# Hybrid decoder layer on one core: other places in the engine queues for evacuations, copies, bias splits and gates, and a weight remainder in four instructions

## The reference, cut to what matters

```python
h = rms_norm(x, g_mix[l])
proj = h @ w_in[l] + b_in[l]          # q, k, v, r, g_lr | sq, sk, sv | gate_a, gate_b
log_g = log_sigmoid(g_lr @ w_gla_gate[l] + b_gla_gate[l]) / GLA_TAU
o_a = gla_chunked(gq, gk, gv, log_g)
o_a = o_a * rsqrt(mean(o_a * o_a) + NORM_EPS) * g_gla_head[l]
y_a = (o_a * silu(gr)) @ w_gla_out[l]
y_b = swa_with_sinks(rope(sq), rope(sk), sv, sinks[l]) @ w_swa_out[l]
mixed = sigmoid(gate_a) * y_a + sigmoid(gate_b) * y_b
x = x + mixed @ w_out[l]
x = x + moe_ffn(rms_norm(x, g_ffn[l]), w_router[l], b_router[l], w_e1[l], b_e1[l], w_e2[l], b_e2[l])
return rms_norm(x, g_final)
```

## Time and profile before

| what | us |
|---|---|
| median of 3 runs | 1237.48 |
| lowest, highest | 1231.65, 1239.58 |
| profiled execution, its own time | 1239.21 |
| span of its instructions | 1237.4 |
| TensorE busy (matmul) | 1136.9 |
| VectorE, ScalarE, GpSimd busy | 375.1, 267.7, 123.4 |

### The profile page before, as it was taken

The page is one execution under the profiler, slowest core; times in us unless marked ns, Lnnn a source line. Parts: engine busy times, 40 slices in busy tenths (PEclk is TensorE's granted clock), DMA queues, the critical chain, the costliest instruction groups (busy, mean ns, idle before and its releaser), DMA issues.

```text
span 1237.4 us, 17251 instructions
## 1 busy us (share of the span) xinstructions
PE 1136.9 (92%) x7218; PEld 564.4 (46%) x7218; DVE 375.1 (30%) x620; ACT 267.7 (22%) x405; POOL 123.4 (10%) x42
## 2 busy tenths in 40 slices
PE   6979999998999999999889889999999999999986
PEld 5978789986433333333333333333333333333332
DVE  6786663694411121111111111122111111111112
ACT  5446564423111111111111111111111111111112
POOL 6332462432000000000000000000000000000000
PEclk9989999999999999999999999999999999999999
DMA  7533323948999999999999999999999999999995
GB/s 297 196 136 123 129 107 120 365 158 323 367 386 427 431 426 427 428 426 430 428 428 429 427 429 427 431 426 430 430 427 430 427 431 426 430 430 427 429 427 215
DMA packets 35825, 448.13 MB, mean 362 GB/s; under 512 B 4160, under 2 KB 4288, under 8 KB 6576
## 3 DMA queue, kind: packets, MB, share of 16 engines
q1 hardware_dynamic: 34992, 445.99, 86.5%
q0 software_dynamic: 368, 1.24, 0.3%
q10 hardware_dynamic: 432, 0.42, 0.1%
HBM read 446.58 MB, written 1.05 MB: 362 GB/s over the span
## 4 chain that ended last, share of the span: by engine, by line
DMA 44%; PE 42%; DVE 8%; issue 2%; ACT 2%; POOL 1%; SPq 0%; DVEq 0%; ACTq 0%
DMA ring<-wexp 44%; PE PS L817 23%; PE PS L557 9%; PE PS L810 3%; PE PS L802 2%; PE PS L874 1%; ACT slot_R L918 1%; DVE slot_R L1149 1%; PE PS L653 1%; DVE EXT L1187 1%; DVE slot_R L1169 1%; PE PS L869 0%; DVE EXT L1218 0%; DVE BRW L1185 0%; DVE BE L1186 0%
## 5 line engine op out<-in xcount | busy, mean ns | idle before, releaser
L817 PE MATMUL PS<-ring,SQ 128*64 128x512 f32 x2016 | 455.0, 596 | 61.7 <-DMA ring<-wexp 61.4
L817 PEld LDWEIGHTS PS<-ring,SQ 128*64 128x64 f32 x2016 | 138.3, 136 | 352.9 <-issue 227.3
L817 PE MATMUL PS<-ring,PTG 128*64 128x512 f32 x1024 | 226.8, 595 | 0.0
L817 PEld LDWEIGHTS PS<-ring,PTG 128*64 128x64 f32 x1024 | 70.7, 137 | 152.2 <-issue 133.2
L1562 DVE TENSOR_SCALAR SQ<-PS 128x512 f32<-128x512 f32 x32 | 22.1, 692 | 364.9 <-PE PS L817 364.9
L1096 ACT ACTIVATE SQ<-SQ 128x512 f32<-128x512 f32 x32 | 20.2, 630 | 500.6 <-DVE SQ L1562 500.6
L487 POOL TENSOR_TENSOR slot_R<-ring,slot_R 128x2048 fp32r<-128x2048 f32 (+1 forms) x20 | 98.3, 4916 | 148.4 <-ACT slot_R L918 148.3
L1553 DVE TENSOR_TENSOR PTG<-TAB,GR 128x128 bf16<-128x128 f32 x32 | 9.4, 292 | 333.8 <-PE PS L862 333.8
L557 PE MATMUL PS<-slot_R 128*128 128x256 f32 (+1 forms) x296 | 95.4, 322 | 0.0
L918 ACT ACTIVATE slot_R<-ring 128x2048 fp32r<-128x2048 f32 (+1 forms) x38 | 71.8, 1890 | 44.0 <-PE PS L557 21.9
L557 PE MATMUL PS<-HT_R,slot_R 128*128 128x256 f32 x400 | 76.4, 293 | 4.9 <-ACT ring L956 2.8
(11 more groups left out here) (264 smaller groups left out, 977.0 us busy)
## 6 DMA issues: line engine op xcount, KB each, us to landing
ring<-wexp SPq DMA_DIRECT2D x190, 2048.0 KB, 33.4
ring<-wblk SPq DMA_DIRECT2D x36, 1024.0 KB, 4.9
EXT<-wexp SPq DMA_DIRECT2D x2, 2048.0 KB, 9.1
BRW<-brow SPq DMA_DIRECT2D x7, 256.0 KB, 5.0
ring<-wskv SPq DMA_DIRECT2D x2, 768.0 KB, 11.3
EXT<-x SPq DMA_DIRECT2D x2, 512.0 KB, 4.5
out<-EXT SPq DMA_DIRECT2D x3, 256.0 KB, 2.0
EXT<-gfin POOLq DMA_DIRECT2D x1, 512.0 KB, 9.4
```

The costliest lines, as they stand in the source:

```text
L817: last = mm(PS[g * SLOTS:(g + 1) * SLOTS, b, :], lhsT, rhs[:, g * 512:(g + 1) * 512], start=start, stop=stop)
```

## The change

Arithmetic, matmul count and loads stay. What changes place:

1. GpSimd computes each weight remainder in four instructions of a quarter's width instead of one.
2. The first block's matmuls go contraction step by step over both halves, and wait for the transposed input by pairs of steps; in its second unit the product with the weight remainder comes before the one with the input's remainder.
3. VectorE: `rest(4)`, `rest(6)`, `rest(8)` each come after an evacuation; the decay exponents leave their place ahead of the transposed copies and go to the attention slots 0 and 1; in slot 8 `swa_pt(7)` comes ahead of `swa_out(6)`.
4. ScalarE: the evacuation of block gq comes ahead of the Exp and Ln of the gate; the last two decay exponentials go from slot 1 to slot 2.
5. The gate of r: piece 16 is done on GpSimd ahead of unit 21's remainder, piece 17 on VectorE (`gr_last`) after unit 22's remainder.
6. Bias splits: part 0 of be1 comes ahead of `rest(30)`; part 1 of be1 goes from after results 28 and 29 to after results 26 and 27.

```diff
             for u in range(NU):
+                if u == 21:
+                    gr_finish(16)
                 if by_pool(u):
                     pool.wait_ge(hi_ready, u + 1)
-                    nc.gpsimd.tensor_tensor(w_unit(u, True), w_unit(u), h_unit(u, True).bitcast(F32),
-                                            ALU.subtract).then_inc(lo_p, 1)
+                    quarter = unit_width(u) // 4
+                    for n in range(4):
+                        part = slice(n * quarter, (n + 1) * quarter)
+                        last = nc.gpsimd.tensor_tensor(w_unit(u, True)[:, part], w_unit(u)[:, part],
+                                                       h_unit(u, True)[:, part].bitcast(F32), ALU.subtract)
+                    last.then_inc(lo_p, 1)
...
-                if u == 21:
-                    gr_finish(16)
-                    gr_finish(17)
...
             def first_block():
 
                 banks = [pj_bank(), pj_bank()]
+                terms = (((0, 0), (1, 0), (0, 1)), ((0, 0), (0, 1), (1, 0)))
                 for u in range(2):
-                    for a, b in ((0, 0), (1, 0), (0, 1)):
+                    for term, (a, b) in enumerate(terms[u]):
                         if a + b == 0:
                             pe.wait_ge(hi_ready, u + 1)
-                            pe.wait_ge(ht_hi, 2 * (u + 1))
-                        elif a:
-                            pe.wait_ge(ht_ready, 2 * (u + 1))
-                        else:
+                        elif b:
                             split_done(pe, u)
                         w = (h_unit(u, True), w_unit(u, True))[b]
-                        for half in range(2):
-                            for k in range(KH):
+                        for k in range(KH):
+                            if k % 2 == 0 and a + b == 0:
+                                pe.wait_ge(ht_hi, 2 * u + k // 2 + 1)
+                            elif k % 2 == 0 and a:
+                                pe.wait_ge(ht_ready, 2 * u + k // 2 + 1)
+                            for half in range(2):
...
             split(10)
+            feature_major(3, [GQT[:, c * BW:(c + 1) * BW] for c in range(2)], C_BQ, ACT.Identity)
 
             act.wait_ge(gate_neg, 1)
             link(fn(W1, W0, ACT.Exp))
             fn(W1, W1, ACT.Ln, bias=1.0).then_inc(gate_sp, 1)
-            feature_major(3, [GQT[:, c * BW:(c + 1) * BW] for c in range(2)], C_BQ, ACT.Identity)
...
                 if n == 1:
-                    decays()
+                    block_decays()
+                if n == 2:
+                    near_decays()
...
-            act.wait_ge(gr_ready, 4)
+            act.wait_ge(gr_ready, 3)
+            act.wait_ge(gr_last, 1)
             feature_major(9, MIX[0:2], C_BGA, ACT.Sigmoid)
...
-                if m and u < 5:
-                    rest(u + 5)
+                if 0 < u < 4:
+                    rest(2 * u + 2)
             rotate_queries(1)
...
+                if n == NGRP:
+                    swa_pt(n - 1)
                 if n - 2 >= 0:
                     swa_out(n - 2)
-                if 0 <= n - 1 < NGRP:
+                if 0 <= n - 1 < NGRP - 1:
                     swa_pt(n - 1)
...
+                if n == 0:
+                    block_exponents()
+                elif n == 1:
+                    near_exponents()
...
+            dve.wait_ge(gr_sig, 4)
+            g = GR[:, 1, BW:D]
+            link(v.tensor_tensor(g, g, SIG[:, BW:D], ALU.mult))
+            gv = g.rearrange("p (h d) -> p h d", h=2)
+            v.tensor_tensor(gv, gv, ROW[:, R_HEAD:R_HEAD + GDV].unsqueeze(1).broadcast_to([P, 2, GDV]),
+                            ALU.mult).then_inc(gr_last, 1)
             rest_t(OB2, obt_full, obt_lo)
...
             rest_t(OA2, oat_full, oat_lo)
+            biases1(0)
             rest(30)
...
-                biases(i - 13)
+                biases2(i - 13)
+                if i == 13:
+                    biases1(1)
                 rest(2 * i + 6)
```

More of the change, by code:

```diff
@@ L597, in first_block @@
                 banks = [pj_bank(), pj_bank()]
+                terms = (((0, 0), (1, 0), (0, 1)), ((0, 0), (0, 1), (1, 0)))
                 for u in range(2):
-                    for a, b in ((0, 0), (1, 0), (0, 1)):
+                    for term, (a, b) in enumerate(terms[u]):
                         if a + b == 0:
                             pe.wait_ge(hi_ready, u + 1)
-                            pe.wait_ge(ht_hi, 2 * (u + 1))
-                        elif a:
-                            pe.wait_ge(ht_ready, 2 * (u + 1))
-                        else:
+                        elif b:
                             split_done(pe, u)
                         w = (h_unit(u, True), w_unit(u, True))[b]
-                        for half in range(2):
-                            for k in range(KH):
+                        for k in range(KH):
[4 more added lines that the diff above has]
+                            for half in range(2):
                                 last = mm(bk(banks[half]), HT2[a][:, KH * u + k, half * P:(half + 1) * P],
-                                          w[:, k * BW:(k + 1) * BW], start=(u + a + b + k == 0),
-                                          stop=(u == 1 and b == 1 and k == KH - 1), skip_group_check=True)
-                            if b == 1 and (u or half):
-                                last.then_inc(pj_full[banks[half]] if u else first_used, 1)
+                                          w[:, k * BW:(k + 1) * BW], start=(u + term + k == 0),
+                                          stop=(u == 1 and term == 2 and k == KH - 1), skip_group_check=True)
+                                if term == 2 and k == KH - 1 and (u or half):
+                                    last.then_inc(pj_full[banks[half]] if u else first_used, 1)
             first_block()
@@ L1001, in gr_sigmoid, with block_decays @@
                 fn(SIG[:, m * BW:(m + 1) * BW], GR[:, m, n * BW:(n + 1) * BW], ACT.Sigmoid).then_inc(gr_sig, 1)
-            def decays():
+            def block_decays():
                 v0 = W0.rearrange("p (h t) -> p h t", h=GH)
@@ L1012, in decays, with near_decays @@
                     fn(w, w, ACT.Exp, scale=1.0 / TAU).then_inc(decay_out, 1)
+            def near_decays():
                 act.wait_ge(decay_in, 4)
@@ L1176, in _ @@
             rest(2)
-            rest(4)
             def bias_part(part, dst, raw, base, done):
@@ L1187, in bias_part, with biases1, biases2 @@
                     link(v.tensor_tensor(raw, raw, places[0], ALU.subtract))
-            def biases(part):
+            def biases1(part):
                 dve.wait_ge(be1_in, 16)
                 bias_part(part, BE1, BE1R, 0, be1_ready)
+            def biases2(part):
                 dve.wait_ge(be2_in, 16)
@@ L1405, in _ @@
             link(v.reciprocal(S_GRS, S_GSD))
-            dve.wait_ge(gr_ready, 4)
+            dve.wait_ge(gr_ready, 3)
+            dve.wait_ge(gr_last, 1)
             for h in range(GH):
@@ L1444, in _ @@
                 if i == 15:
-                    biases(2)
+                    biases1(2)
+                    biases2(2)
                     v.memset(Y, 0.0).then_inc(y_ready, 1)
```

6 lines of the change are left out of this document (3 added, 3 removed).

## The result

The changed kernel takes 1219.19 us (median of 4 runs, 1218.33 to 1219.72) against 1238.53 (4 runs, 1231.65 to 1239.89) of the kernel before beside it: ratio 0.9856, 95% interval 0.9826 to 0.9885. That is faster by over 1%. The profiled execution has a span of 1217.3 us, 20.1 less than before, where the sum had 14.1. The spans miss by 6.0 us and the times by 4.2 because the profiled execution before lay 1.7 above the median that the forecast started from.

What follows compares the result with a forecast made beforehand. From about 320 us the unchanged expert-weight DMA stream bounds the kernel, so earlier TensorE gains move the end one for one. Six terms sum to 15.1 us, less 1.0: 14.1, so 1223.4 us against 1237.5; range 1216 to 1232.

Steps and rivals of the forecast that it cites:

- Rival B: GpSimd against VectorE: the shared port pair isn't freed between quarters; net 3.3 us worse, 1226.7 us; chance 12%.
- Term 1: First blocks: result 0's wait and clock loss go (+4.0), less 0.8 and 1.2 of new waits; taken as +1.8 us.
- case with a lowered clock: Within the first blocks' sum: if the first block's wait, near 2 us, lowers the clock too, 1.2 us of gain remain.
- Terms 2 and 3: Block gq's evacuation no longer behind Exp and Ln, +4.5 us; transposed copies no longer behind the decay exponents, +6.4 us.
- Term 3: Transposed copies: with the decay exponents gone from ahead, wait 3.6 and clock loss 2.8 go, +6.4 us.
- Term 4: Attention: slot 4's wait of 2.0 and clock 1.7 go, plus 1.0 in slot 8; +4.7 us.
- rival C: Attention slots 2, 4 and 5: three waits of 1.2 us and twice the clock, 7 us, 1230.4 us; chance 23%.
- the reserve of 1.0: 1.0 us taken off the sum for slots 2, 4 and 5, where the walk left under half a microsecond.
- Term 5: Gate of r: the wait on block ga0's evacuation grows from 1.9 to 3.0 us, clock lost as before; -1.1 us.
- Term 6: Bias splits: part 0 waits for be1's load, results 26 and 28 come late; new 5.8 against old 4.6, -1.2 us.
- rival A: Bias splits: be1 lands early or the wait is short, so +4 instead of -1.2; 1218.2 us; chance 15%.

Runs made afterwards that it cites:

- the run with eighths: Changed kernel with each GpSimd remainder in eight instructions of 256 columns instead of four: 1222.33 us, ratio 0.9879 to the kernel before.
- the quarters alone: Kernel before with the GpSimd remainders in four instructions each and nothing else changed: 1227.31 us, ratio 0.9914.
- the moves alone: Changed kernel with each GpSimd remainder in one instruction again, all else as changed: 1224.39 us, ratio 0.9898 to the kernel before.
- the old order of products: Changed kernel with the input's remainder again ahead of the weight's in the first block's second unit: 1218.84 us, ratio 0.9849 to the kernel before.
- the old gate: Changed kernel with gate pieces 16 and 17 both on GpSimd behind unit 21's remainder, as before the change: 1220.57 us, ratio 0.9858 to the kernel before.

## Why the prediction was right, and where its sum was off

**The frame held.** What TensorE gains before the expert stage moves the end by nearly as much: 21.3 us at new x, 20.9 at the first gather, 20.1 at the end.

**The quarters: right in kind.** One quarter of wait for a VectorE instruction (1.25 us at most), 5.0 us for a unit alone: measured about 1.0 to 1.13 and 5.02. Rival B, where the pair isn't freed between quarters, fell: no VectorE instruction waits for more than one quarter, and the run with eighths shows the same alternation at half the grain. What I didn't draw from it is that quarters are a different share of the pair. I wrote "The total that GpSimd blocks is no smaller; it is handed out in pieces" and walked most stretches as before. Where VectorE's row is dense and GpSimd's queue long, the pieces slow the row to 1.7 us an instruction (those of the row that read PSUM excepted); where TensorE waits for VectorE's next instruction alone, they are all gain.

**Term 1, the step that failed: "`rest(4)` no longer stands ahead of the evacuation of result 0 ... +4.0. Against it: ... the first block ends 0.8 later ... a wait of 1.2 us more than before."** The gain of 4.0 came, and it has two causes, each enough by itself: with the quarters alone TensorE reaches the gate input at 50.30, with the moves alone at 49.84, with both at 50.71, against 54.91 before. Neither of the two costs came out of the sum. The first block's wait on unit 1's remainder is there (1.6 us), but the sum put at nothing what the new waits by pairs of steps give: the first product starts at 11.90 instead of 12.90 and the old waits of 1.8 and 0.6 shrink to 0.5, so unit 2 starts at 24.84 where it was 24.82. The quarters do cost there: with whole remainders in the new order unit 2 starts at 23.69. The evacuation of skv's result was walked to 48.8 and came at 47.17, a wait of 0.2. The prediction's case with a lowered clock ("1.2 remain") doesn't follow from its own numbers, 2.0 less 1.7 being 0.3; nothing hung on it, as the clock behind the wait is 1.00.

**Terms 2 and 3 held**, 4.5 and 6.3 against 4.5 and 6.4, and putting block gq's evacuation back costs 4.5. (With quarters alone the same wait, 2.7 us, cost no clock: last section.) Term 3's number is right as a step between the two kernels, but it is not what the move is worth in the new one: 11.1, half because the quarters make the old place slower, half because the other moves bring TensorE there sooner. The working gave the wait of the kernel before, and that is what a difference between two kernels needs; the price of undoing a part needs the new timing.

**Term 4 held** (4.7, and rival C's three hopping waits didn't come, the reserve of 1.0 with them). The product that was shut out for 4.54 us met one quarter. With whole remainders and the moves a wait of 1.5 us on slot exponentials is still there, and with quarters alone both old waits, 2.0 and 1.0, are gone though `swa_pt(7)` keeps its place. So this term is largely the quarters'; what the order in slot 8 is worth by itself no run shows.

**Term 5 held**, 3.3 us of wait against a forecast 3.0: one quarter was met, as worked, but by the first product behind `rest(22)` (L1407 took 1.74 us) and not by `rest(22)` itself (2.39). Its clock was lost as charged: the window behind it has 0.64 over 4.76 us.

```profile
158.24:163.00 4.76, 4.76 (x27) 4.76 (x28) 0.00 (x0) 2.48 (x3) 2.21 (x2) 0.64 0.00 0
...
234.25:240.00 5.75, 5.75 (x48) 5.75 (x49) 5.65 (x4) 1.92 (x1) 5.75 (x5) 1.00 0.26 74
```

**Term 6, the step that failed: "GpSimd's unit 31 (from 240.67) takes 5.0 out of it ... So TensorE stands still for 0.7 and then 3.4 us and loses 1.7 to the clock."** be1's load bound part 0 as forecast: the cast starts at 213.85 behind 8.15 us of idle, and result 26 is 0.6 us late (forecast 0.7). But unit 31 isn't taken whole out of VectorE's time. Ahead of result 28 VectorE waited for three quarters: 1.68, 3.26 and 3.27 us for instructions that take 0.68, 2.28 and 2.29, 3.0 us in all; the last of the three ends at 233.6 and the two results behind it, which read PSUM, aren't held. The wait was 1.4 instead of 3.4, and behind it the clock stayed at 1.00 (second row above), so 1.7 more weren't lost. 2.0 of wait against the 5.8 foreseen. With the moves alone, where unit 31 is whole, result 28 does wait 2.8 us and the clock behind it is 0.72 over 6 us: the step was nearly right for whole remainders, and it was the quarters that it left out. And against the old place the new one is worth nothing, by the run with the biases put back: the term's gain is the quarters' as well. The time came out 1.0 us above rival A's 1218.2. be1 wasn't early; what came true of rival A is a short wait, for a cause that it doesn't name. That is the 4.1 us of the miss, besides 2.4 in term 1, 1.0 of reserve and -0.4 in terms 3 and 5; 14.1 + 7.1 = 21.2, which is what TensorE has gained at new x.

**The range** of 1216 to 1232 leaves room for how close this term is: in two kernels that leave this stretch of code alone (the old order of products, the old gate) the wait on result 28 is 2.4 us, since unit 31's quarters start 1.5 to 1.9 us earlier and VectorE meets a fourth.

## What to carry to other kernels

Where one engine locks another out for a whole instruction, cutting the long instruction is a cheaper edit than moving the short ones out of its way: four pieces cost 0.4 us per unit and gave 11 us on the old order, without a look at where each wait was; all the moves together gave 14. Look first which instructions are locked out at all: here those that read PSUM never were, so the ones to protect are those ahead of an evacuation. But it pays only where a single instruction of the other engine is urgent. A row of short instructions slows down by one piece each, and the piece engine by one instruction each, so cut no finer than the urgent wait asks (eight pieces lost 3 us again), and keep such rows away from a long queue of pieces.

Value an edit on the timing that the other edits leave, not on the old one: the exponents' move is worth 6 us alone and 11 beside the rest of the change, the remainders' and the biases' moves nothing clear of the noise beside it.

## What the runs showed of the hardware that was not expected

The pair changes hands after each instruction even in a row of GpSimd instructions without a semaphore between them. A wait behind a quarter doesn't depend on the size of what waits: a product of 4 columns is held for 1.05 us (1.21 instead of 0.16), one of 512 for 1.13 (1.82 instead of 0.69), and copies on 32 partitions too (1.68 for a 0.68 us copy of be1's part 1). VectorE instructions that read PSUM aren't held (468 of 468).

The start isn't the same in every execution. In four of the fourteen traces TensorE's first eight matmuls take 3.75 us, in the others some 2.1. The run with both gate pieces ahead of unit 21, then the changed kernel:

```profile
12.12 3.75 PE L616 MATMUL PS<-slot_R,HT_R 128*128 128x512 f32 x8 [0.54 <-ACT HT_R L945]
```

```profile
11.90 2.09 PE L615 MATMUL PS<-slot_R,HT_R 128*128 128x512 f32 x8 [0.55 <-ACT HT_R L944]
```

The wait on unit 1's remainder takes this up (unit 2 starts at 25.08 and 24.84), so a missing 1.6 us in a wait list isn't a gain by itself. Why they are slow stays open; the granted clock reads 1.00 in both.

A wait of TensorE has no fixed price in clock. I charged 1.7 us to each of about 2 us or more. The same wait on result 28 cost it in one kernel and not in another. TensorE's wait from 233 to 240 us and the window, first with the old order of products, then with the old gate:

```profile
PE PS L560 <- DVE EXT L1452: 2.4, 1, 2.4
```

```profile
234.00:240.00 6.00, 5.18 (x43) 5.18 (x44) 5.90 (x6) 1.92 (x1) 5.70 (x4) 1.00 0.15 37
```

```profile
PE PS L561 <- DVE EXT L1445: 2.4, 1, 2.4
```

```profile
234.00:240.00 6.00, 4.82 (x28) 4.82 (x29) 5.90 (x6) 0.37 (x1) 6.00 (x4) 0.72 0.01 3
```

Clock 1.00 (2.4 GHz) throughout in the first, a fall toward 1.2 GHz in the second, 0.28 x 6.0 = 1.7 us, with the same wait and the same code around it. Longer and shorter waits do both too. The wait on block gq's evacuation of 2.8 us was followed by 0.62 in the kernel before; one of 2.7 us at the same place, with quarters alone, by this window:

```profile
63.85:70.00 6.15, 6.15 (x51) 6.15 (x52) 4.64 (x5) 4.49 (x5) 3.60 (x2) 1.00 0.30 93
```

In the kernel with the exponents alone moved, TensorE waits 1.53 us on a slot's exponentials to 109.6 and 1.36 us to 128.4; the windows behind them:

```profile
109.60:115.00 5.40, 5.39 (x23) 4.22 (x24) 4.22 (x13) 5.24 (x11) 0.00 (x0) 0.68 0.33 140
128.40:134.00 5.60, 5.60 (x31) 4.44 (x32) 4.03 (x5) 2.22 (x2) 3.72 (x1) 1.00 0.34 143
```

The first lost 0.32 x 5.4 = 1.7 us, the second nothing. The waits of 3.3 to 3.4 us on block ga0's evacuation were followed by a lower clock in every kernel that had them, for 1.7 us or so, with eighths for 2.9 (0.50 over 5.75 us). From 1.5 to 2.8 us of wait the price is thus close to 1.7 us or nothing, and what decides between them stays open. The longer waits on the query copies, 3.6, 4.1 and 8.2 us, cost more: 2.8 us before the change, 2.5 with quarters alone (0.29 x 8.47) and 3.1 with the exponents back (0.34 x 9.14).
